# LRU pairs written out, and VectorE merging each pair inside the next one

## The reference, cut to what matters

```
xc = causal_conv(lx, width 4)
r  = sigmoid(blockdiag(xc, w_a) + b_a);   i = sigmoid(blockdiag(xc, w_i) + b_i)
log_a = -8 * r * softplus(-lam);          a = exp(log_a)
u  = sqrt(-expm1(2*log_a)) * i * xc       # factor 1 at position 0
h_t = a_t * h_(t-1) + u_t
y_lru  = h * gelu(ly)
merged = gm0*y_mlstm + gm1*y_gla + gm2*y_lru          # gm = sigmoid(mgate)
x = x + merged @ w_out
```

## Time and profile before

| | |
|---|---|
| median of 3 executions | 3452.79 us (3448.68, 3452.79, 3452.84; the middle one is the median) |
| the profiled execution's own time | 3447.87 us |
| its span in the trace | 3446.1 us |
| TensorE busy, of the span | 3320.0 us, 96% |
| VectorE busy | 1891.7 us, 55% |
| ScalarE busy | 1014.6 us, 29% |
| chain that ended last, by engine | PE 80%, DVE 9%, ACT 6%, issue 4%, DMA 1% |
| mean granted clock of TensorE | 0.96 |

### The profile page before, as it was taken

One profiled execution on the slowest core, in us unless ns is written; L12 is line 12 of the kernel. 1 busy time (PEld: TensorE's weight loads), 2 busy tenths in 40 slices (PEclk: granted clock), 3 DMA queues, 4 the chain that ended last, 5 costly groups with the idle time before them and its releaser, 6 DMA issues.

```text
span 3446.1 us, 59571 instructions
## 1 busy us (share of the span) xinstructions
PE 3320.0 (96%) x25040; PEld 3245.3 (94%) x25040; DVE 1891.7 (55%) x2523; ACT 1014.6 (29%) x962; POOL 0.4 (0%) x9
## 2 busy tenths in 40 slices
PE   7999999999999889999999999999999998899997
PEld 7999989989999889999999999899899998899997
DVE  5434455556767775434444345555666677654344
ACT  4212322222332553212232123222332245432122
POOL 0000000000000000000000000000000000000000
PEclk9999989999999999999999999999999999999999
DMA  3222222232222122222222222222222222222222
GB/s 128 84 101 81 90 77 88 93 110 85 75 76 81 68 73 84 83 91 85 79 93 82 95 84 87 89 108 104 75 77 85 75 72 78 74 87 74 97 76 72
DMA packets 52053, 294.27 MB, mean 85 GB/s; under 512 B 9080, under 2 KB 12280, under 8 KB 23032
## 3 DMA queue, kind: packets, MB, share of 16 engines
q1 hardware_dynamic: 37296, 242.48, 20.6%
q10 hardware_dynamic: 14672, 50.60, 4.0%
HBM read 271.55 MB, written 21.50 MB: 85 GB/s over the span
## 4 chain that ended last, share of the span: by engine, by line
PE 80%; DVE 9%; ACT 6%; issue 4%; DMA 1%; DVEq 0%; ACTq 0%
PE stream_b L358 32%; PE stream_a L358 32%; PE stream_a L432 5%; PE mix L457 2%; ACT wh L703 2%; PE stream_b L432 1%; PE mix L465 1%; PE mix L515 1%; PE mix L608 1%; DVE wl L968 1%; PE mix L517 1%; PE mix L506 1%; DVE wS L1311 1%; DMA out_o_ss<-CS 1%; DVE rstd L993 1%
## 5 line engine op out<-in xcount | busy, mean ns | idle before, releaser
L703 ACT ACTIVATE wh<-stage 128x2048 fp32r<-128x2048 f32 (+2 forms) x246 | 436.2, 1774 | 814.8 <-PE stream_b L358 590.3
L968 DVE TENSOR_TENSOR wl<-stage,wh 128x2048 fp32r<-128x2048 f32 (+2 forms) x248 | 525.9, 2121 | 170.7 <-ACT wh L703 152.8
L358 PE MATMUL stream_a<-xh,wh 128*128 128x272 f32 x2560 | 553.1, 298 | 62.8 <-DVE lxs L1358 32.0
L358 PE MATMUL stream_a<-xl,wh 128*128 128x272 f32 x2560 | 542.0, 294 | 0.0
L358 PE MATMUL stream_a<-xh,wl 128*128 128x272 f32 x2560 | 542.0, 294 | 0.0
L358 PE MATMUL stream_b<-xh,wh 128*128 128x272 f32 x2560 | 536.7, 291 | 2.3 <-DVE xg L1073 2.3
L358 PE MATMUL stream_b<-xl,wh 128*128 128x272 f32 x2560 | 529.7, 288 | 0.0
L358 PE MATMUL stream_b<-xh,wl 128*128 128x272 f32 x2560 | 527.7, 288 | 0.0
L358 PEld LDWEIGHTS stream_a<-xh,wh 128*128 128x128 f32 x2560 | 417.1, 195 | 74.9 <-DVE lxs L1358 33.7
L358 PEld LDWEIGHTS stream_a<-xh,wl 128*128 128x128 f32 x2560 | 416.5, 195 | 0.0
L358 PEld LDWEIGHTS stream_b<-xh,wh 128*128 128x128 f32 x2560 | 403.4, 188 | 11.4 <-issue 5.3
(11 more groups left out here) (304 smaller groups left out, 4767.4 us busy)
## 6 DMA issues: line engine op xcount, KB each, us to landing
stage<-in_w_up SPq DMA_DIRECT2D x88, 1024.0 KB, 4.8
stage<-in_w_mix SPq DMA_DIRECT2D x88, 1024.0 KB, 4.8
stage<-in_w_down SPq DMA_DIRECT2D x32, 768.0 KB, 4.2
stage<-in_w_down SPq DMA_DIRECT2D x32, 640.0 KB, 3.9
seven<-rows_scratch ACTq DMA_DIRECT2D x8, 1088.0 KB, 8.0
CS<-in_c ACTq DMA_DIRECT2D x8, 1024.0 KB, 4.6
out_o_sc<-CS ACTq DMA_DIRECT2D x8, 1024.0 KB
CS<-in_s ACTq DMA_DIRECT2D x8, 1024.0 KB, 4.8
```

The costliest lines, as they stand in the source:

```text
L358: mm = [pe.matmul(out(h), a(h), b(h), start=f, stop=z) for h in range(2)]
L703: act.activation(wh[:, slot, 0:width], stage[:, slot, 0:width], ACT.Copy).then_inc(hi_done, 1)
L968: tt_(wl[:, slot, 0:width], stage[:, slot, 0:width], wh[:, slot, 0:width].bitcast(F32), ALU.subtract).then_inc(split_done, 1)
```

## The change

Three edits, in ScalarE's and in VectorE's stream. First, the loops over the pairs are written out on both engines, so that every position is a constant. Second, on VectorE the merges of a pair are not done at its end: merge 0 of a pair comes behind `conv(0)` of the next, and merge 1 behind its `take_y(0)`; the last pair's merges follow it as before, and the memset with its wait on `lru_done` is done once a layer in place of once a pair. Third, ScalarE's `gates(j)` waits until the merge of j of the pair before is done, since its tanh writes `tt`. TensorE's stream is the same instruction for instruction.

```diff
@@ ScalarE, gates(j) of lru_pair @@
                     act.wait_ge(l_ri, k + 1)
+                    if i * 2 + j2:
+                        act.wait_ge(m_ready, k - 1)
                     act.activation(halves(rr[:]), banks(Q[:, 0:2]), ACT.Sigmoid, bias=V[:, ds(g + V_BA, 1)])
@@ ScalarE, mix @@
-                with act.Fori(0, KT // 4) as i:
+                for i in range(KT // 4):
...
-                act.wait_ge(lru_done, L * (KT // 2) + KT // 2 + 1)
+                act.wait_ge(lru_done, L + 2)
@@ VectorE, lru_pair(L, i, j2, before) @@
                 take_x(0)
                 conv(0)
+                if before:
+                    before(0)
                 take_x(1)
                 split(2)
                 conv(1)
                 take_y(0)
+                if before:
+                    before(1)
                 recur(0)
...
-                for v in range(2):
+
+                def merge(v):
...
-                dve.memset(t8[:], 0.0).then_inc(lru_done, 1)
-                dve.wait_ge(lru_done, pr + 2)
+
+                return merge
@@ VectorE, mix @@
-                with dve.Fori(0, KT // 4) as i:
-                    lru_pair(L, i, 0)
-                    lru_pair(L, i, 1)
+                merge = None
+                for i in range(KT // 4):
+                    for j2 in range(2):
+                        merge = lru_pair(L, i, j2, merge)
+                merge(0)
+                merge(1)
+                dve.memset(t8[:], 0.0).then_inc(lru_done, 1)
+                dve.wait_ge(lru_done, L + 2)
```

More of the change, by code:

```diff
@@ L1342, in gla_head, with lru_pair @@
                 link(tt_(Hh[:], Hh[:], Gm[:], ALU.mult))
-            def lru_pair(L, i, j2):
+            def lru_pair(L, i, j2, before):
                 pr = L * (KT // 2) + i * 2 + j2
```

## The result

The changed kernel takes 3415.72 us, the median of four runs (3412.85 to 3416.85), against 3450.73 for the kernel before (four runs, 3447.02 to 3452.84): a ratio of 0.9898, interval 0.9886 to 0.9910, 35.0 us less. The profiled execution took 3412.85 us; its span is 3411.1 us against 3446.1, also 35.0 less.

The account below looks back on a forecast made before the run. VectorE's pair of 46.29 us, longer than TensorE's 40.3, was taken as the bound. Gains of 15.3 and 14.1 us in the layers plus 1.8 ahead, taken as 31, gave 3421 us; range 3412 to 3438.

Parts of the forecast that it names:

- The boundary wait: TensorE's wait for `take_x(0)` before tile 2 of the next pair, 5 to 6 us, was to go.
- The new cycle, 42.08: Time from one `recur(0)` to the next: 20.04 + 2.21 + 19.83 = 42.08 us, above TensorE's 40.3.
- the first leg: VectorE from `take_x(0)` to `recur(0)`, now holding the merges: 21.54 us less 1.71 for 19 register rows, 19.83.
- The second leg: From `recur(0)` to `split(4)`, paced by ScalarE: 20.33 us less a 0.29 wait for tile 5, 20.04.
- The front, 0.9 us a layer: Ahead of a layer's first `recur(0)`, the convolutions' ten gaps save about 0.9 us a layer, 1.8 in all.
- The sum of the stages, 31.1: Both layers' gains from first `recur(0)` to last merge, 29.3 us, plus 1.8 ahead of it: 31.1.
- TensorE's wait at tile 5, 1.8 us in the last two pairs: TensorE waits at tile 5 for `take_y(1)`, which stands behind `recur(0)`: 42.08 - 40.3 = 1.8 us a pair.
- The wait added on ScalarE, zero: `gates(0)` waiting for merge 0 of the pair before costs zero: met by 1 us, tanh with 5 to spare.
- The last term, a longer idle ahead of the last merge: TensorE idles some 3 us more before the output projection; not priced, at most another slow stretch of a few us.
- The rival that the gaps stay: Writing out brings nothing on VectorE, only the order does: cycle 44.08 us, gains 15.5, time 3437; chance 0.17.
- The rival by the clock: TensorE's clock falls at tile 5; two slow stretches a pair lose 1 to 3 us per cycle: 3430 to 3439; chance 0.10.
- The rival by late code: More written-out VectorE code could bring stops of 0.37 us each; 80 would eat the gain; no separate chance given.

Follow-up runs that it names:

- the steps put back: The changed kernel with one VectorE register step put back at each place in the pair where the loops had one: 3432.24 us, ratio 0.9947.
- the kernel that traded it for others: The changed kernel with `take_y(1)` put ahead of `recur(0)`: 3424.61 us, ratio 0.9929.
- the kernel with the merges together: The changed kernel with merge 0 moved from behind `conv(0)` to directly ahead of merge 1, in front of `recur(0)`: 3425.87 us, ratio 0.9927.
- the written-out kernel: The kernel before with only VectorE's and ScalarE's loops over the pairs written out, merges still at a pair's end: 3436.39 us, ratio 0.9966.

## Why the prediction was right

3421 was predicted, 3415.72 measured; 31 us of gain, 35.0 measured, of which 32.7 lie in the stages, where the mechanism works. The other 2.3 are luck: the rest of the span moves by more than that from profile to profile. Step by step:

- **The boundary wait goes, and nothing of its size comes in its place.** Right. Six waits of 4.3 to 6.4 us went, and with them the fall of the clock at each. One of the six is the 5.98 of the earlier trace rows.
- **The new cycle, 42.08.** Measured 41.8 in five of the six cycles of the profile, 42.13 in one. The term that was off is the saving in the first leg: 1.71 us predicted, for 19 register rows of 0.09, and 21.54 - 19.53 = 2.0 measured. The price of a row was right: the steps put back cost 1.70 of this leg. The other 0.3 went with the loop but is more than single rows cost; some gaps of the kernel before were wider, as the 0.20 ahead of `conv(0)`, and what fills them was not tested. The second leg, 20.04 predicted, is 20.02 in the first pair and 20.39 in the second.
- **A layer from the first `recur(0)` to the last merge's end, 155.60.** Measured 1269.23 - 1114.37 = 154.86 and 2953.60 - 2799.13 = 154.47.
- **The front, 0.9 us a layer.** Measured 15.97 - 15.20 = 0.8 (1104.14 to 1120.11 before, 1099.17 to 1114.37 after), and 0.8 in the second layer.
- **The sum of the stages, 31.1.** Measured 32.7.
- **TensorE's wait at tile 5, 1.8 us in the last two pairs.** Measured 2.13 and 1.75 in the first layer; the clock fell behind the second of them for a few us, and `recur(0)` of no pair waited for it. In the changed kernel this wait costs nothing, and the kernel that traded it for others was slower.
- **The wait added on ScalarE, zero.** Right, with 1.4 us to spare where 1 had been worked out (with 31.3 for the merge, where its own terms, 20.04, 2.21 and 9.3, make 31.5); the kernel with the merges together shows what it costs when the spare time is used up.
- **The last term, a longer idle ahead of the last merge.** It was 5.3 us in either layer, 0.7 more than before, not 3 more: the two waits of 2.84 and 2.50 stand where 1.77 and 2.88 did, and TensorE reaches the projection 6.3 us ahead of the last merge's end in the first layer, where it was 5.6. This term was left out of the sum on a guess that was too large; leaving it out did no harm.
- **The rival that the gaps stay** falls twice, by the written-out kernel and by the register rows put back. With it falls what the Trainium skill ("VectorE: DVE Perf Modes", "The DRAIN you can't avoid") would make of these gaps: inside all 16 merges 0.03 to 0.04 us are left between two dependent VectorE instructions, and a register step puts back 0.09.
- **The rival by the clock** needed two long falls in every pair; ahead of the last merges one short fall is there in the first layer and none in the second.
- **The rival by late code.** Its price, 0.37 a stop, was right: no gap over 0.04 stands inside a merge, but one stop of 0.37 is there in the first layer, the one ahead of `split(4)` at 1176.53 that makes the cycle of 42.13. It comes back at the same place when the kernel runs again. That the code came late there is not shown, only that VectorE started 0.47 behind the high part with nothing else to wait for in the rows. One such stop is far from the 80 that the rival needed.
- **What no step held** is the 2.3 us outside the stage. The part ahead of the first stage runs the same instructions and was 5.0 us shorter; its stretches at 0.50 came to 99.0 us against 116.1. In the other profiles of this study that part has 92 to 113 us of them and the rest of the span moves between 3070 and 3081 us. So the 2.3 can't be put down to the change.

In the changed kernel ScalarE and VectorE together set the pace; that the second leg is ScalarE's is shown by the run that moved one of ScalarE's instructions and won 17 us of the stages.

## What to carry to other kernels

When two engines take turns, draw the cycle as legs with the engine that owns each, and price a move by the leg it leaves and the one it enters: here the merges left the leg in which TensorE stood still and entered one in which it was already served. A wait that appears on the busiest engine need not cost anything; look at who owns the cycle before removing it. And after one leg is shortened look at the other's owner: one instruction of ScalarE's, put ahead of a gelu and two sigmoids, then gave another 0.6%. The same move in the kernel before gave 0.4%; there the merges waited for the sigmoids it had put back.

## What the runs showed of the hardware

- A register step between two dependent VectorE instructions costs 0.09 us (0.76 against 0.85 from start to start); the 19 in the leg that VectorE owns made 1.7 us of it (21.23 against 19.53).
- The granted clock fell to 0.50 at each of TensorE's six waits of 4.3 to 6.4 us in the kernel before. In the changed kernel it stayed full behind a wait of 2.13 and fell behind one of 1.75; when the same kernel ran again, it fell behind the 2.12 at the same place. So the length of the last wait does not tell it alone.
- The part of the span that no edit touched took 3070 to 3081 us; it was shortest where TensorE had stood at the lower clock for 225 to 227 us of it, and longest at 253 us.
